# Gated DeltaNet chunks of a decoder block: chunks written out, filler set product by product, waits and three steps reordered

## The reference

```python
A = where(strict, (k * beta) @ k.T * decay, 0)          # per chunk and head
T = inverse(eye + A)                                    # unit lower triangular
u = T @ (v * beta);  w = T @ (k * beta * exp(gc))
attn_qk = (q @ k.T) * decay
v_new = u - w @ state
o = (q * exp(gc)) @ state + attn_qk @ v_new
state = state * exp(g_last) + (k * exp(g_last - gc)).T @ v_new
...
y = sc_b * conv3(sc_c * sc_h)                           # short convolution
```

## Time and profile before

| | |
|---|---|
| runs | 2924.07, 2922.69, 2923.04 us; median 2923.04 |
| span of the profiled execution | 2921.6 us (it has no other time of its own; 1.4 us below the median of the runs) |
| granted clock of TensorE | 0.998 |
| PE busy | 2881.8 us, 99% |
| DVE, ACT, POOL busy | 64%, 39%, 51% |

### The profile page before, as it was taken

The page is one execution under the profiler, slowest core; times in us unless marked ns, Lnnn a source line. Parts: engine busy times, 40 slices in busy tenths (PEclk is TensorE's granted clock), DMA queues, the critical chain, the costliest instruction groups (busy, mean ns, idle before and its releaser), DMA issues.

```text
span 2921.6 us, 43014 instructions
## 1 busy us (share of the span) xinstructions
PE 2881.8 (99%) x14070; PEld 2394.2 (82%) x14070; DVE 1859.1 (64%) x2636; ACT 1145.3 (39%) x2049; POOL 1479.3 (51%) x1214
## 2 busy tenths in 40 slices
PE   8999999999999999999999999999999999999998
PEld 8888788888888888887888878888888888888786
DVE  2565566655359777777877556665634866665778
ACT  5532545434234333334543254443423433333334
POOL 7422455452226555568972244445322655555886
PEclk9999999999999999999999999999999999999999
DMA  7522222151113444467643232224111222224764
GB/s 260 209 96 102 94 80 72 61 177 51 58 72 114 165 152 163 165 222 246 228 144 144 100 109 73 72 65 166 65 44 74 82 108 108 97 93 146 260 192 169
DMA packets 179210, 372.41 MB, mean 127 GB/s; under 512 B 17104, under 2 KB 58128, under 8 KB 179088
## 3 DMA queue, kind: packets, MB, share of 16 engines
q1 hardware_dynamic: 116592, 301.06, 29.6%
q10 hardware_dynamic: 62496, 69.78, 7.0%
HBM read 268.51 MB, written 102.27 MB: 127 GB/s over the span
## 4 chain that ended last, share of the span: by engine, by line
PE 93%; DVE 2%; DMA 1%; POOL 1%; issue 1%; ACT 1%; SPq 0%; DVEq 0%; ACTq 0%; POOLq 0%
PE PS L3018 21%; PE PS L3020 21%; PE PS L3019 21%; PE PS L1991 2%; PE PS L1995 2%; PE PS L1993 2%; PE PS L1964 2%; PE PS L1962 2%; PE PS L1963 2%; PE PS L1875 2%; PE PS L3056 2%; PE PS L3052 2%; PE PS L3054 2%; PE PS L1897 2%; PE PS L3034 1%
## 5 line engine op out<-in xcount | busy, mean ns | idle before, releaser
L3018 PE MATMUL PS<-act_hi,w_hi 128*128 128x512 f32 (+1 forms) x1080 | 424.9, 393 | 1.0 <-POOL w_lo L2327 0.7
L774 POOL TENSOR_TENSOR down_lo<-down_raw,down_hi 128x1024 fp32r<-128x1024 f32 (+1 forms) x196 | 390.8, 2029 | 49.5 <-ACT down_hi L1248 49.2
L3020 PE MATMUL PS<-act_hi,w_lo 128*128 128x512 f32 (+1 forms) x1080 | 403.1, 373 | 0.0
L3019 PE MATMUL PS<-act_lo,w_hi 128*128 128x512 f32 (+1 forms) x1080 | 402.0, 372 | 0.0
L2352 POOL TENSOR_TENSOR w_lo<-raw,w_hi 128x256 fp32r<-128x256 f32 (+1 forms) x144 | 209.4, 1477 | 357.0 <-ACT w_hi L2447 357.0
L740 POOL TENSOR_TENSOR part_lo<-sum_s,part_hi 128x512 fp32r<-128x512 f32 x176 | 235.3, 1344 | 226.8 <-ACT part_hi L1228 226.3
L1705 DVE TENSOR_TENSOR copied<-copied,PS 128x512 f32<-128x512 f32 x264 | 177.4, 686 | 230.9 <-PE PS L3020 221.6
L3018 PE MATMUL PS<-op_t_hi,part_hi 128*128 128x512 f32 x704 | 274.4, 390 | 0.3 <-issue 0.2
L3020 PE MATMUL PS<-op_t_hi,part_lo 128*128 128x512 f32 x704 | 273.9, 389 | 0.0
L3019 PE MATMUL PS<-op_t_lo,part_hi 128*128 128x512 f32 x704 | 273.9, 389 | 0.0
L1789 DVE TENSOR_TENSOR h<-h,PS 128x512 f32<-128x512 f32 x344 | 218.1, 678 | 62.3 <-PE PS L3020 43.6
(11 more groups left out here) (368 smaller groups left out, 6432.1 us busy)
## 6 DMA issues: line engine op xcount, KB each, us to landing
raw<-in_w_units SPq DMA_DIRECT2D x132, 512.0 KB, 3.9
a_d<-copied SPq DMA_DIRECT2D x154, 256.0 KB, 2.2
down_raw<-a_d SPq DMA_DIRECT2D x154, 256.0 KB, 3.6
gu_raw<-in_w_units SPq DMA_DIRECT2D x44, 512.0 KB, 4.7
down_raw<-t_d SPq DMA_DIRECT2D x88, 256.0 KB, 3.0
down_raw<-in_w_units SPq DMA_DIRECT2D x66, 256.0 KB, 3.0
qkvz_d<-stage ACTq DMA_DIRECT2D x64, 256.0 KB, 2.5
raw<-att_d SPq DMA_DIRECT2D x32, 512.0 KB, 3.2
```

The source lines that it names most:

```text
L774: last = pool.tensor_tensor(flat(lo[:, :, :])[:, cs], flat(down_raw[m % 4][:, :, :])[:, cs], flat(hi[:, :, :])[:, cs].bitcast(f32), ALU.su ...
L3018: nc.tensor.matmul(out_ap, whi, xhi, start=start, stop=False)
L3019: nc.tensor.matmul(out_ap, whi, xlo, start=False, stop=False)
L3020: return nc.tensor.matmul(out_ap, wlo, xhi, start=False, stop=stop)
```

## The change

- The loop of three turns is replaced by its chunks written out, on PE, DVE, ACT and POOL.
- Filler is counted in single products instead of slices of three, by four tables (`FILL_FIRST`, `FILL_SECOND`, `FILL`, `FILL_LAST`). More products stand in chunk 0 (88) and fewer in chunk 1 (56).
- On PE the order of steps becomes gram, value transposes (with their own filler ahead and behind), a1t, levels, y6, w, x6, v, o.
- On DVE the `vb` update comes ahead of level 6's subtraction, and `output_scale` behind the two products with the gram.
- Where an instruction has several waits, the one expected last is put last.
- The norm sums go to PSUM banks 5 and 6, the even blocks' transposes always to bank 2. ACT's second copy `c_out` is moved to y4 in chunk 0.

```diff
@@ -167,11 +167,15 @@
 
 
 STEPS = ["load", "start", "gram", "a1t"] + [f"{x}{l}" for l in range(1, LEVELS) for x in "yx"] + list("wvo")
-FILL = [0, 0, 2, 2] + [2, 1] * 6 + [2, 0, 0]
-FILL_LAST = [0, 0, 2, 2] + [2, 1] * 6 + [2, 0, 0]
-FILL_FIRST = [0, 6, 0, 2] + [1, 1] * 6 + [2, 1, 1]
-CHUNK_SLICES = 3 * NCH * KT // 2
-assert sum(FILL) == sum(FILL_FIRST) == CHUNK_SLICES
+PE_STEPS = ["start", "gram", "vt", "a1t"] + [f"{x}{l}" for l in range(1, LEVELS - 1) for x in "yx"] + \
+    ["y6", "w", "x6", "v", "o"]
+PAIR_PRODUCTS = 9 * NCH * KT
+FILL = [0, 2, 3, 7] + [6, 5, 6, 5, 5, 5, 6, 5, 6, 1] + [1, 3, 5, 1, 0]
+FILL_FIRST = [18, 2, 2, 9] + [6, 4, 6, 4, 6, 4, 6, 4, 6, 2] + [0, 3, 5, 1, 0]
+FILL_SECOND = [0, 2, 2, 6] + [5, 4, 5, 4, 4, 4, 5, 4, 5, 0] + [0, 2, 4, 0, 0]
+FILL_LAST = [0, 2, 3, 7] + [6, 5, 6, 5, 5, 5, 6, 5, 6, 5] + [0, 2, 4, 0, 0]
+FILLS = [FILL_FIRST, FILL_SECOND] + [FILL] * (TT - 3) + [FILL_LAST]
+assert all(sum(FILLS[m] + FILLS[m + 1]) == PAIR_PRODUCTS for m in range(0, TT, 2))
 
 
 def block_kernel(nc, x, mem, w_units, w_ab, conv_w, sc_w, a_log, dt_bias, gdn_g, sc_g,
...
@@ -1024,7 +1028,7 @@
                     act.wait_ge(S["sc_full0"], R * 3 + 1)
                     act.wait_ge(S["sc_halo_out"], R)
                     act.activation(sc_u[:, 2:2 + CH], bank(0), ACT.Copy).then_inc(S["c_out"], 1)
-                if par == 0 and step == "y6":
+                if par == 0 and step == ("y4" if first else "y6"):
                     act.wait_ge(S["sc_full1"], R * 3 + 1)
                     act.activation(sc_u[:, 2 + CH:2 + 2 * CH], bank(1), ACT.Copy)\
                         .then_inc(S["c_out"], 1)
...
@@ -1488,14 +1492,14 @@
                 l = int(step[1]) if step[0] in "yx" else 0
                 if step == "gram":
 
-                    if not first:
-                        output_scale(dve, n - 1)
+                    dve.wait_ge(S["decm_ready"], n * 3 + 3)
                     dve.wait_ge(S["gram_full"], n + 1)
-                    dve.wait_ge(S["decm_ready"], n * 3 + 3)
                     dve.tensor_tensor(two(am0[:, :, :]), gram[:, :, :, 0, :], two(am0[:, :, :]),
                                       ALU.mult).then_inc(S["am0_ready"], 1)
                     dve.tensor_tensor(two(A[:, 0, :, :]), gram[:, :, :, 0, :], two(A[:, 0, :, :]),
                                       ALU.mult).then_inc(S["a_ready"], 1)
+                    if not first:
+                        output_scale(dve, n - 1)
                 if step == "a1t":
 
                     dve.wait_ge(S["vt_full"], n + 1)
...
@@ -1515,16 +1519,6 @@
                 if step == "y1":
                     dve.tensor_tensor(two(A[:, 1, :, :]), gram[:, :, :, 1, :], two(A[:, 1, :, :]),
                                       ALU.mult).then_inc(S["attn_ready"], 1)
-                if step[0] == "x":
-
-                    dve.wait_ge(S["xy_full"], n * 6 + l)
-                    dve.wait_ge(S["x_ready"], n * LEVELS + l)
-                    dve.tensor_tensor(
-                        odd_blocks(Xm[:, :, :], l), odd_blocks(Xm[:, :, :], l),
-                        bank(4)[:, 0:NH * P // 2].rearrange("p (m c) -> p m c", c=1 << l),
-                        ALU.subtract).then_inc(S["x_ready"], 1)
-                    if l < LEVELS - 1:
-                        even_columns(dve, n, l + 1)
                 if step == "x6":
 
                     dve.wait_ge(S["ks_full"], n + 1)
@@ -1534,6 +1528,16 @@
                             G["nbeg"][:, bass.ds(m, 1), hh:hh + 1].rearrange("p n h -> p (n h)"),
                             vb[:, hh, :], ALU.mult, ALU.add)
                     last_rest.then_inc(S["vrest_ready"], 1)
+                if step[0] == "x":
+
+                    dve.wait_ge(S["x_ready"], n * LEVELS + l)
+                    dve.wait_ge(S["xy_full"], n * 6 + l)
+                    dve.tensor_tensor(
+                        odd_blocks(Xm[:, :, :], l), odd_blocks(Xm[:, :, :], l),
+                        bank(4)[:, 0:NH * P // 2].rearrange("p (m c) -> p m c", c=1 << l),
+                        ALU.subtract).then_inc(S["x_ready"], 1)
+                    if l < LEVELS - 1:
+                        even_columns(dve, n, l + 1)
                 if step == "x1":
 
                     if par == 0 and not first:
...
@@ -1847,30 +1851,28 @@
                                          kqn[:, hh, :, :].rearrange("p s t -> p (s t)"),
                                          start=True, stop=True)
                 t.then_inc(S["gram_full"], 1)
-                pe.wait_ge(S["s_ready"], n * 4)
+            if step == "vt":
                 if first:
 
                     pe.wait_ge(S["ld0"], n * 24 + 48)
                     pe.wait_ge(S["stage_ready"], (half + 1) * NH * 8)
                     for b in (2, 3):
                         pe.wait_ge(S[f"qkvz_out{b}"], (half + 1) * NH * CONV_OUT_PER[b])
+                pe.wait_ge(S["s_ready"], n * 4)
                 for hh in range(NH):
                     t = nc.tensor.transpose(r4(bank(3))[:, hh, :], vv[:, par, hh, :], ident[:, :])
                 t.then_inc(S["vt_full"], 1)
             if step == "a1t":
+                pe.wait_ge(S["scln_ready"], R * 2 if par == 1 or first else R * 2 - 1)
                 pe.wait_ge(S["am0_ready"], n + 1)
-
-                pe.wait_ge(S["scln_ready"], R * 2 if par == 1 or first else R * 2 - 1)
                 for hh in range(NH):
                     t = nc.tensor.transpose(r4(bank(2))[:, hh, :], am0[:, hh, :], ident[:, :])
                 t.then_inc(S["a1t_full"], 1)
             if step[0] == "y":
-                pe.wait_ge(S["x_ready"], n * LEVELS + l)
-                pe.wait_ge(S["am_ready"], n * 6 + l)
                 if l == 1:
                     pe.wait_ge(S["vb_ready"], n + 1)
-                else:
-                    pe.wait_ge(S["ym_ready"], n * 12 + 2 * (l - 1))
+                    pe.wait_ge(S["am_ready"], n * 6 + l)
+                pe.wait_ge(S["x_ready"], n * LEVELS + l)
                 for q in range(2):
                     t = nc.tensor.matmul(
                         bank(3)[:, q * P:(q + 1) * P].rearrange("p (m c) -> p m c", c=1 << l),
...
@@ -1900,10 +1902,8 @@
             if step == "w":
 
                 pe.wait_ge(S["s_ready"], n * 4)
-                if last:
-                    pe.wait_ge(S["oo_ready"], n)
-                else:
-                    pe.wait_ge(S["rln_ready"], n + 2)
+                pe.wait_ge(S["kdec_ready"], n + 1)
+                pe.wait_ge(S["oo_ready"], n)
                 for hh in range(NH):
                     t = nc.tensor.matmul(r4(bank(7))[:, hh, :], kqn[:, hh, 0, :], state[:, hh, :],
                                          start=True, stop=True)
...
@@ -1938,14 +1938,12 @@
                 pe.wait_ge(S["kdec_ready"], n + 1)
                 transpose_o(pe, n - 1)
             if step == "x5" and not last:
-                if first:
-                    pe.wait_ge(S["kdec_ready"], n + 1)
-                else:
-                    pe.wait_ge(S["oo_ready"], n)
+                pe.wait_ge(S["scln_ready"], R * 2)
                 sums_norm(pe, n + 1)
             if step == "y3" and par == 0 and not first:
-                sc_sums(pe, R - 1, 1)
+                sc_sums(pe, R - 1, 1, 6)
             if step == "o" and par == 1 and not last:
+                pe.wait_ge(S["rln_ready"], n + 2)
                 sc_sums(pe, R, 0)
 
         def att_scores(pe, half, hp, t):
...
@@ -3370,12 +3359,12 @@
 
                     R = half * 4 + j
                     n_u = unit(half, U_MIX + j * 3)
-                    done = par * CHUNK_SLICES
-                    for step, fill in zip(STEPS, FILL_FIRST if first else FILL_LAST if last else FILL):
+                    done = sum(FILLS[m - 1]) if par else 0
+                    for step, fill in zip(PE_STEPS, FILLS[m]):
                         chunk_step_pe(pe, half, m, par, j, step, first, last)
                         for s in range(done, done + fill):
-                            u, c, k = s // (NCH * KT), s // KT % NCH, s % KT
-                            if k == 0:
+                            u, c, k, i = s // (3 * NCH * KT), s // (3 * KT) % NCH, s // 3 % KT, s % 3
+                            if k == 0 and i == 0:
                                 if c == 0:
                                     pe.wait_ge(S["w_lo_ready"], n_u + u + 1)
 
@@ -3385,16 +3374,17 @@
                                     pe.wait_ge(S["c_out"], R * 2 + c + 1)
                                 else:
                                     pe.wait_ge(S["u_ready"], R * 2 + c + 1)
-                            product = col_slice(PS[:, c, :], u, c, k)
-                            if k == KT - 1:
+                            ks, cs = slice(k * P, (k + 1) * P), slice(c * CH, (c + 1) * CH)
+                            product = nc.tensor.matmul(
+                                PS[:, c, :], (w_lo if i == 2 else w_hi)[u][:, ks],
```

(41 more changed lines are left out.)

20 lines of the change are left out of this document (11 added, 9 removed).

## The result

| | before | after |
|---|---|---|
| median (range) of the runs timed in turn, us | 2922.69 (2921.11 to 2924.07) | 2933.43 (2932.34 to 2933.9) |
| span of the profiled execution, us | 2921.6 | 2931.7 |
| granted clock | 0.998 | 0.998 |

The change makes the kernel slower: the ratio is 1.0034, with an interval of 1.0024 to 1.0045. The forecast was 2918, with a range of 2905 to 2927.

What follows compares the result with a forecast made beforehand. PE, busy 99%, was taken as the bound, with 28.5 us of hidden waits. Per half +3.2, -3.4, 0, -0.7, +2.6 and +0.5 gave +2.2; twice that plus 0.3 is 4.7 us, from 2923.04 to about 2918, range 2905 to 2927.

Steps and rivals of the forecast that it cites:

- chain of POOL's masks: Even chunks: POOL splits a weight tile, then makes decay masks; last ends at y6 + 11.86, unmoved by filler.
- even chunks: Ends of chunks 2, 4, 6: y1 at y6 + 15.46; each loses 1.1 us, wins 0.87 inside; -0.7 per half.
- product 96: First filler product of the third weight tile, in chunk 1; waits on DVE's sc_u, starts at y6 + 16.57.
- loops' price: x to y takes 1.22 us in unlooped chunk 7, 1.38 in looped chunks; straight code saves register operations.
- four small operations of output_scale (558.39 to 559.18, 0.79 us): DVE work now between am0 and y1, priced at 0.79 us; am0 to y1's input Xm grows from 2.55 to 3.34.
- odd chunks: Chunks 3 and 5: win 0.87 us inside each and 0.45 at each end, nearly no wait; +2.6 per half.
- behind chunk 1: End of chunk 1: shorter tail of 18 products gives back 0.2 us, cancelling the 0.2 gained inside.
- chunk 0 into 1: Passage between chunks: y1 at y6 + 17.0, wait grows from 0.6 to 4.0 us, losing 3.4 per half.
- The rule: DVE with two SBUF inputs and GpSimd take a shared port pair in turn; POOL loses 1.0 us in its chain.
- POOL's chain grows: Rival, chance 0.14: DVE's normalising meets all POOL's pieces and masks, 1.0 us more at eight ends; 2926.
- The fill covers nearly all: Rival, chance 0.22: DVE no longer meets POOL's pieces, even ends 1.0 us shorter; 2910, or 2902 without the filler wait.
- Waits only move: Rival, chance 0.12: each wait a product leaves returns at the next step, the chunk's serial chain stays; 2923.

Runs made afterwards that it cites:

- experiment 4: Kernel before the change, only its loops of three turns replaced by written-out chunks on PE, DVE, ACT and POOL: 2917.55 us, ratio 0.9980.
- experiment 3: Changed kernel with one more wait: POOL's first block mask waits until output_scale, kept in its new place, has ended: 2917.73 us, ratio 0.9983.
- experiment 1: Changed kernel with only the move of output_scale undone, back ahead of am0 on DVE: 2916.43 us, ratio 0.9981.
- experiment 5: experiment 4 with output_scale moved behind the two gram products: 2926.91 us, ratio 1.0014 against the kernel before.
- experiment 6: experiment 1 with ACT's rounding of the next weight tile 0 moved from y6 to y5 in even chunks: 2907.23 us, ratio 0.9945.
- experiment 7: experiment 6 with four filler products moved from chunk 0 to chunk 1 (84 and 60): 2902.11 us, ratio 0.9930.
- experiment 2: Changed kernel with two filler products of chunk 1 moved from behind a1t to behind y1: 2935.18 us, ratio 1.0037.

## Why the prediction was wrong

**Right.** PE is the bound. Inside the chunks the waits went as forecast: y-steps follow their product after 0.23 us, and 0.07 of wait per chunk is left. The chain of POOL's masks was right to 0.03 us. y6 of chunk 4 starts at 482.71:

```profile
482.71 0.60 PE L1877 MATMUL PS<-Xm,am 128*128 128x128 f32 x4
...
489.16 0.49 PE L1928 MATMUL PS<-vnew,dec 128*128 128x128 f32 x2 [0.19 <-ACT vnew L1082]
```

The masks end at 493.25 + 1.29 = 494.54, y6 + 11.83 (forecast 11.86), and am0 starts at y6 + 11.86 (forecast 11.96). In chunk 1 am0 came at y6 + 11.39 (forecast 11.48). PE waits where it was said to: a1t and y1 in even chunks, product 96 in chunk 1. The loops' price was there too: writing them out alone is worth 6.5 us (experiment 4).

**Wrong: "four small operations of output_scale (558.39 to 559.18, 0.79 us)".** The duration was read in the place that the change takes them from, where only the first of them still meets POOL. In before, at the start of chunk 7, the last mask ends at 558.65, and `ost_u` takes 0.27 us from 558.39 to just behind it:

```profile
557.38 1.27 POOL L697 TENSOR_TENSOR dec<-dec,upto 128x512 f32<-128x512 f32 x1
```

By themselves the four take 0.67 or 0.68 (experiment 3). In the new place they cost 1.75. The missing 0.96 us stands at the start of every chunk but the first of a half, 14 in all. With other slips, read from start to start, it makes:
- even chunks, 6 ends: y1 at y6 + 16.25, forecast 15.46, so 0.8 more. The waits are 2.5 for 1.7: 0.35 for v's result at the o-part (the second row above), 0.6 at a1t and 1.5 at y1. It is less than 0.96 because the other links came out some hundredths shorter each, as POOL's semaphore, forecast 0.1 and measured 0.03.
- odd chunks, 4 ends: forecast none, measured 1.1. Here a second slip adds to the first. I asked whether DVE is ready for a1t, and it is: am0 starts at y6 + 11.40, against 12.6. I didn't follow the chain on to y1. By my own links, 11.40 + 3.34 + 0.16 = 14.90, and PE's work reaches y1 at 14.64 (y1 at 463.30 less y6 at 447.53, less the 1.13 waited). So 0.26 us would have been waited even at 0.79.
- behind chunk 1, 2 ends: y1 stands at y6 + 15.78 too, though four products fewer stand ahead of it. The forecast comes to 16.27 - 9 x 0.232 + 0.2 = 14.4, so 1.4 more. Of it 0.7 is a wait of the value transposes for DVE's `state` (L1863 on L1591), which the prediction did not have.
- chunk 0 into 1, 2 places: product 96 at y6 + 17.35, forecast 16.57, and y1 at 17.89, forecast 17.0: 0.9 more.

Together 6 x 0.8 + 4 x 1.1 + 2 x 1.4 + 2 x 0.9 = 13.8 us, and 1.5 from the clock in half two (below): 15.3. The stages waited 38.3 where the forecast left 28.5 - 4.7 = 23.8, so 14.5 are to be explained. The pieces agree within a microsecond, and the profiled execution shows each of them at every end of its kind within 0.15 us.

Experiments 1, 3 and 5 show the cause from three sides. Undoing the move, and keeping POOL away from it, gives 17.0 and 15.7 us back; the move in the other kernel costs 9.4. That 17 is more than 14 x 0.96 = 13.4, because in experiment 1 all four operations leave the chain from am0 to y1, and not only what POOL adds to them. The two profiled executions split the stages' 16.0 us: six even ends 1.1 each, four odd ends 0.8 each, chunk 0 into 1 1.4 in each half, chunk 1 with its end 2.5 in both halves together (the fall of the clock is in here), and 0.9 inside the other chunks. Experiment 3 leaves the four where they are, so its 15.7 are the better price of the meeting, the clock and product 96 included.

**The rule.** The prediction weighed the port of DVE and POOL, and set it against POOL's weight pieces only. The small operations on DVE meet the block masks, and the price falls on DVE. The Trainium skill, SBUF — State Buffer, "SBUF: two separate sides", says that the pair is held for the whole instruction and that the other engine blocks fully. The rows agree: an operation of 0.16 us that starts 0.03 after a mask takes 0.74, the mask's length. For DVE the section names two SBUF inputs or a two-port mode. `ost_w` is a TENSOR_SCALAR of four columns with one tensor in, so it can fall under the second alone, and it takes 0.67. Whether it runs in such a mode no row shows.

**The rivals.** "POOL's chain grows" was right on the sign and on meetings as the cause, and wrong on place and engine: POOL's chain kept its length. "The fill covers nearly all" needed POOL's pieces out of the way, which the change doesn't do; experiments 6 and 7 do it, with the scale back in its old place, and get 2907 and 2902. "Waits only move" was closer than its 0.12: without the move of the scale, the filler and the new order win nothing beyond the written-out loops (experiments 1 and 4), since what leaves the levels of an even chunk comes back at its end. A theory formed after the result, that written-out code itself costs, fell with experiment 4; another, that too little filler at the chunk's end was the cause by itself, fell with experiments 3 and 5, which change no filler and take nearly all of the loss away or bring more than half of it back.

**Open.** The first stage opens 2.03 us later in after (311.98) than before (309.95), ahead of all that the change touches in it. In experiments 1 to 3, whose code is the same up to there, it opens at 309.58, 308.02 and 309.87. So I hold this for variation between profiled executions; what varies wasn't looked into.

## What to carry to other kernels

Price a moved operation by what runs beside it in its new place: ask above all which engine the instruction ahead of it releases. Follow a chain to its last consumer (y1), not to the first (a1t). Before more filler is put at a wait, look for what holds the releaser: here rounding one tile a step sooner won 9.2 us, and the other fill about 5. Filler that is taken from one wait to cover another wins only what the first can spare.
